# Strassen's scheme for the feed-forward down products: seven block products in place of eight

## The reference, cut to what matters

```python
def sq_relu_mlp(h, w_up, w_down):
    return jnp.square(jax.nn.relu(h @ w_up)) @ w_down
...
D_FF_2 = -(-8 * D_MODEL // (3 * 256)) * 256
```

## Time and profile before

| | |
|---|---|
| timed runs | 2347.6, 2345.95, 2345.96 us; median 2345.96 us |
| span of the profiled execution | 2345.8 us |
| TensorE busy | 2331.8 us (99%), 11493 matmuls |
| VectorE, ScalarE, GpSimd busy | 705.7, 935.1, 1079.8 us (30%, 40%, 46%) |
| chain that ended last | TensorE 96% |
| mean granted TensorE clock | 0.998 of 2.4 GHz |

### The profile page before, as it was taken

One profiled execution on the slowest core, in us unless ns is written; L12 is line 12 of the kernel. 1 busy time (PEld: TensorE's weight loads), 2 busy tenths in 40 slices (PEclk: granted clock), 3 DMA queues, 4 the chain that ended last, 5 costly groups with the idle time before them and its releaser, 6 DMA issues.

```text
span 2345.8 us, 29181 instructions
## 1 busy us (share of the span) xinstructions
PE 2331.8 (99%) x11493; PEld 1932.6 (82%) x11493; DVE 705.7 (30%) x1174; ACT 935.1 (40%) x1867; POOL 1079.8 (46%) x888
## 2 busy tenths in 40 slices
PE   9999999999999999999999999999999999999998
PEld 8888888888878888888887888888898778888887
DVE  3424320223474310323446321001242564100113
ACT  5525432333674432433446233223233662332331
POOL 5533644443535444544454354444454504544443
PEclk9999999999999999999999999999999999999999
DMA  6321333332303333323320243333333203433332
GB/s 189 86 63 54 117 99 95 99 96 72 99 30 108 102 99 95 99 92 92 93 89 32 91 132 94 101 97 98 91 104 77 75 1 91 129 101 95 99 96 75
DMA packets 156943, 213.73 MB, mean 91 GB/s; under 512 B 33615, under 2 KB 81479, under 8 KB 156807
## 3 DMA queue, kind: packets, MB, share of 16 engines
q1 hardware_dynamic: 153424, 203.24, 28.8%
q10 hardware_dynamic: 3383, 8.62, 1.2%
HBM read 209.18 MB, written 2.10 MB: 90 GB/s over the span
## 4 chain that ended last, share of the span: by engine, by line
PE 96%; DVE 1%; ACT 1%; issue 1%; POOL 0%; DMA 0%; SPq 0%; DVEq 0%; ACTq 0%; POOLq 0%
PE PS L343 45%; PE PS L345 40%; PE PS L1622 1%; PE PS L1600 1%; PE PS L463 1%; PE PS L2527 1%; PE PS L2514 0%; PE PS L1585 0%; PE PS L2119 0%; DVE X L594 0%; PE PS L1750 0%; PE PS L1150 0%; PE PS L444 0%; PE PS L1749 0%; PE PS L2518 0%
## 5 line engine op out<-in xcount | busy, mean ns | idle before, releaser
L318 POOL TENSOR_TENSOR WL<-WS,WH 128x512 fp32r<-128x512 f32 (+2 forms) x764 | 978.1, 1290 | 1063.5 <-ACT WH L307 1040.1
L307 ACT ACTIVATE WH<-WS 128x512 fp32r<-128x512 f32 (+2 forms) x766 | 473.2, 625 | 1167.4 <-PE PS L343 586.3
L343 PE MATMUL PS<-AH,WH 128*128 128x512 f32 (+1 forms) x1776 | 597.7, 369 | 1.3 <-ACT AH L480 1.3
L343 PE MATMUL PS<-AL,WH 128*128 128x512 f32 (+1 forms) x1776 | 593.5, 366 | 0.5 <-DVE AL L498 0.3
L343 PE MATMUL PS<-AH,WL 128*128 128x512 f32 x1584 | 586.8, 389 | 0.0
L343 PEld LDWEIGHTS PS<-AH,WH 128*128 128x128 f32 x1776 | 309.6, 188 | 57.4 <-issue 2.9
L343 PEld LDWEIGHTS PS<-AL,WH 128*128 128x128 f32 x1776 | 309.8, 189 | 55.7 <-DVE AL L498 0.8
L343 PEld LDWEIGHTS PS<-AH,WL 128*128 128x128 f32 x1584 | 296.9, 188 | 61.6
L345 PE MATMUL PS<-WH,h_HL 128*128 128x512 f32 x864 | 336.1, 389 | 0.0
L345 PE MATMUL PS<-WH,h_HH 128*128 128x512 f32 x864 | 336.1, 389 | 0.0
L345 PE MATMUL PS<-WL,h_HH 128*128 128x512 f32 x864 | 336.1, 389 | 0.0
(11 more groups left out here) (366 smaller groups left out, 1895.5 us busy)
## 6 DMA issues: line engine op xcount, KB each, us to landing
WS<-in_mlp_w_up_dram SPq DMA_DIRECT2D x128, 256.0 KB, 2.8
WS<-in_mlp_w_down_dram SPq DMA_DIRECT2D x128, 256.0 KB, 2.8
WS<-in_ffn_w_gate_dram SPq DMA_DIRECT2D x176, 128.0 KB, 2.1
WS<-in_ffn_w_up_dram SPq DMA_DIRECT2D x176, 128.0 KB, 2.2
WS<-in_ffn_w_down_dram SPq DMA_DIRECT2D x88, 256.0 KB, 2.6
WS<-in_gla_w_in_dram SPq DMA_DIRECT2D x48, 256.0 KB, 2.7
WS<-in_even_w_in_dram SPq DMA_DIRECT2D x48, 256.0 KB, 2.6
WS<-in_odd_w_in_dram SPq DMA_DIRECT2D x32, 256.0 KB, 2.6
```

The lines of the kernel that those rows point to most:

```text
L307: e.activation(WH[:, s, 0:n], WS[:, s, 0:n], ACT.Copy).then_inc(hi.sem, hi.tick(i))
L318: e.tensor_tensor(WL[:, s, 0:n], WS[:, s, 0:n], WH[:, s, 0:n].bitcast(F32), ALU.subtract).then_inc(lo.sem, lo.tick(i))
L343: return e.matmul(PS[b][0:mw, cs], weight[:, s, m * mw:(m + 1) * mw], x[:, cs], start=start, stop=stop, skip_group_check=head is not None)
```

## The change

The down products of the first 3072 hidden features of an MLP and of the first 2048 of an FFN are taken in chunks of 1024 features: 3 and 2 chunks. In a chunk the hidden features (a; 4 quarters of 256 tokens x 512 features) and the weights (b; 4 quarters of 512 rows x 512 columns) form a product of 2x2 blocks, and Strassen's scheme in Winograd's form takes seven products p1 to p7 of sums of them in place of eight. One product is 4 weight blocks x 2 token tiles x 3 matmuls. Some results are left in PSUM and the next product is added to them.

- The weights of a chunk are loaded as they are into a new area `hR` (16 blocks, semaphores `raw`), each as soon as the former chunk has freed its place. The stream has entries without a load (`mixed`) for the 28 blocks of a chunk; ScalarE and GpSimd take their source from `hR`, or from `WS` for p7. VectorE forms the weight differences (`dve_weight_sums`).
- The hidden features of a chunk stay in full precision. VectorE sums quarters (`dve_operand_sums`), ScalarE rounds an operand of 128 x 1024 (`act_op`), VectorE takes its rest (`dve_op`), into two buffers used in turn. Each is listed so that it follows the product two before.
- After each product VectorE adds its two banks to `Y` or `X` (`dve_summed`). In the MLP this was a copy by ScalarE, per column group and token tile.
- The seven products stand in one piece between up groups. MLP: groups 0, 1, 2, chunk 0, 3, 4, chunk 1, 5, two blocks of 6, chunk 2, the rest of 6, 7. FFN: groups 0 to 5, chunk 0, 6, 7, 8, chunk 1, 9, 10. The groups of one period use the same four banks, its products the other four. So in the FFN groups 4 and 5, and 6 and 7, follow each other in the same banks.
- The last 1024 features of an MLP and the last 768 of an FFN go through the same close as before, with 8 and 6 blocks for a column group in place of 16 and 10.

The core of the diff (left out: the buffers' places, the loads of a first chunk, GpSimd's lists, the parts of the MLP that answer to those shown of the FFN, the changed calls):

```diff
-        HH = take("HH", [P, 16, T], F32R)
-        HL = take("HL", [P, 16, T], F32R)
-        HT = take("HT", [P, 2, T])
+        hR = take("R", [P, 4, 4, RW])
...
+            for D, c, b, k in raw_at.get(i, ()):
+                raw_in(e, w, D, c, b, k)
+            if i in mixed:
+                return
...
                 w.wait_ge(mm, "used", i - NS)
+            if i in mixed:
+                source, *at = mixed[i]
+                w.wait_ge(*at)
+                e.activation(WH[:, s, 0:n], source, ACT.Copy).then_inc(hi.sem, hi.tick(i))
+                return
+            w.wait_ge(landed[s], i)
             e.activation(WH[:, s, 0:n], WS[:, s, 0:n], ACT.Copy).then_inc(hi.sem, hi.tick(i))
...
+            source = mixed[i][0] if i in mixed else WS[:, s, 0:n]
+            e.tensor_tensor(WL[:, s, 0:n], source, WH[:, s, 0:n].bitcast(F32), ALU.subtract).then_inc(lo.sem, lo.tick(i))
...
+        PRODUCTS = ("p1", "p7", "p6", "p4", "p5", "p2", "p3")
+        PLACE = {"p1": (0, 0), "p7": (2, 1), "p6": (2, 0), "p4": (2, 0), "p5": (2, 1), "p2": (0, 0), "p3": (0, 1)}
+        OPENS = ("p1", "p7", "p6", "p3")
+        FREED = {"p4": 0, "p5": 1, "p3": 3, "p2": 2}
...
+            def operand(self, q):
+                c, p = q // 7, PRODUCTS[q % 7]
+                if p in ("p6", "p5", "p3"):
+                    p6 = 7 * c + 2
+                    at = {"p6": (ve, "asum", self.name, p6), "p5": (ve, "asum", self.name, p6),
+                          "p3": (ve, "asum", self.name, 7 * c + 6)}[p]
+                    return self.quarter(c, 0, 1 if p == "p5" else 0), at
+                if p == "p7":
+                    return hZ, (ve, "asum", self.name, q)
+                if p == "p1":
+                    return self.quarter(c, 0, 0), self.made(c, 0)
+                return self.quarter(c, 1, 1 if p == "p4" else 0), self.made(c, 1)
...
+        WIDE = {8: (0, 1, 2, 3, 4, 5, 6)}
+        NARROW = {2: (0, 1, 2, 3, 4, 5, 6)}
+        LONG = {16: (0, 1, 2, 3, 4, 5, 6)}
...
+        def weight_source(D, c, p, k, i):
+            if p == "p7":
+                return WS[:, i % NS, :], ve, "wsum", D.name, c, p, k
+            if p in ("p6", "p4", "p5"):
+                return raw_tile(1 if p == "p5" else 0, k), ve, "wsum", D.name, c, p, k
...
+            i0, pair = first[D.name, c, p], banks[2:4] if p in ("p7", "p4", "p2") else banks[0:2]
+            w.wait_ge(ve, "op", D.name, q)
+            for k in range(4):
+                s = (i0 + k) % NS
+                w.wait_ge(lo, i0 + k)
+                for z in range(2):
+                    if k == 0 and held.get(pair[z]):
+                        w.wait_ge(*held[pair[z]])
+                    o, x = PS[pair[z]][:, :], slice(z * P, (z + 1) * P)
+                    xh, xl = D.oh[:, q % 2, k, x], D.ol[:, q % 2, k, x]
+                    e.matmul(o, xh, WH[:, s, :], start=k == 0 and p in ("p1", "p7", "p2"), stop=False, skip_group_check=True)
+                    e.matmul(o, xh, WL[:, s, :], start=False, stop=False, skip_group_check=True)
+                    m = e.matmul(o, xl, WH[:, s, :], start=False, stop=k == 3, skip_group_check=True)
+                    if k == 3:
+                        m.then_inc(mm.sem, mm.tick("product", D.name, q, z))
+                if k < 3:
+                    m.then_inc(mm.sem, mm.tick("used", i0 + k))
+                else:
+                    mm.name("used", i0 + k)
+            for z in range(2):
+                held[pair[z]] = (ve, "summed", D.name, q, z)
...
+        def act_op(e, w, D, q):
+            if q >= 7 * D.n:
+                return
+            source, at = D.operand(q)
+            w.wait_ge(*at)
+            if q >= 2:
+                w.wait_ge(mm, "product", D.name, q - 2, 1)
...
+        def dve_op(e, w, D, q):
+            if q >= 7 * D.n:
+                return
+            w.wait_ge(sc, "op", D.name, q)
+            e.tensor_tensor(D.ol[:, q % 2, :, :], D.operand(q)[0], D.oh[:, q % 2, :, :].bitcast(F32),
+                            ALU.subtract).then_inc(ve.sem, ve.tick("op", D.name, q))
...
+            a11, a21, a12, a22 = D.quarter(c, 0, 0), D.quarter(c, 0, 1), D.quarter(c, 1, 0), D.quarter(c, 1, 1)
+            if p == "p7":
+                w.wait_ge(*D.made(c, 0))
+                e.tensor_tensor(hZ, a11, a21, ALU.subtract).then_inc(ve.sem, ve.tick("asum", D.name, q))
+            elif p == "p6":
+                w.wait_ge(*D.made(c, 1))
+                e.tensor_tensor(a21, a21, a22, ALU.add).then_inc(ve.sem, ve.tick("s1", D.name, c))
+                w.wait_ge(ve, "s1", D.name, c)
+                w.wait_ge(ve, "op", D.name, 7 * c)
+                e.tensor_tensor(a11, a21, a11, ALU.subtract).then_inc(ve.sem, ve.tick("asum", D.name, q))
+            elif p == "p3":
+                w.wait_ge(ve, "op", D.name, 7 * c + 2)
+                e.tensor_tensor(a11, a12, a11, ALU.subtract).then_inc(ve.sem, ve.tick("asum", D.name, q))
...
+                for k in range(4):
+                    i = first.get((D.name, c, p), 0) + k
+                    w.wait_ge(raw[3][k], D.name, c)
+                    w.wait_ge(raw[1][k], D.name, c)
+                    w.wait_ge(lo, i - NS)
+                    e.tensor_tensor(WS[:, i % NS, :], raw_tile(3, k), raw_tile(1, k), ALU.subtract).then_inc(
+                        ve.sem, ve.tick("wsum", D.name, c, p, k))
+            elif p == "p6":
+                for k0 in (0, 2):
+                    b11, b12, b22 = (hR[:, b, k0:k0 + 2, :] for b in (0, 1, 3))
+                    for k in (k0, k0 + 1):
+                        w.wait_ge(raw[0][k], D.name, c)
+                        w.wait_ge(ve, "wsum", D.name, c, "p7", k)
+                    e.tensor_tensor(b12, b12, b11, ALU.subtract).then_inc(ve.sem, ve.tick())
+                    for k in (k0, k0 + 1):
+                        ve.name("wsum", D.name, c, "p5", k)
+                        w.wait_ge(lo, first.get((D.name, c, "p1"), 0) + k)
+                    w.wait_ge(ve, "wsum", D.name, c, "p5", k0)
+                    e.tensor_tensor(b11, b22, b12, ALU.subtract).then_inc(ve.sem, ve.tick())
+                    for k in (k0, k0 + 1):
+                        ve.name("wsum", D.name, c, p, k)
+            elif p == "p4":
+                for k0 in (0, 2):
+                    b11, b21 = hR[:, 0, k0:k0 + 2, :], hR[:, 2, k0:k0 + 2, :]
+                    for k in (k0, k0 + 1):
+                        w.wait_ge(raw[2][k], D.name, c)
+                        w.wait_ge(lo, first.get((D.name, c, "p6"), 0) + k)
+                    e.tensor_tensor(b11, b21, b11, ALU.subtract).then_inc(ve.sem, ve.tick())
+                    for k in (k0, k0 + 1):
+                        ve.name("wsum", D.name, c, p, k)
+        def dve_summed(e, w, D, q, banks):
+            p = PRODUCTS[q % 7]
+            pair, (t0, cg) = banks[2:4] if p in ("p7", "p4", "p2") else banks[0:2], PLACE[p]
+            for z in range(2):
+                t, b = t0 + z, PS[pair[z]]
...
+        def act_period(e, w, D, c, groups, order, closed):
+            for kind, k in walk(8 * len(groups), order):
+                if kind == "product":
+                    for j in range(4):
+                        weight_hi(e, w, first[D.name, c, PRODUCTS[k]] + j + NS)
+                    act_op(e, w, D, 7 * c + k + 2)
+                else:
+                    weight_hi(e, w, first[f"{D.name}.up{groups[k // 8]}", k % 8] + NS)
+                    if k % 8 == 7:
+                        closed(groups[k // 8])
...
+        def dve_period(e, w, D, c, groups, order, closed, banks):
+            late = None
+            for kind, k in walk(8 * len(groups), order):
+                if late is not None:
+                    dve_summed(e, w, D, late, banks)
+                    dve_op(e, w, D, late + 2)
+                    late = None
+                if kind == "product":
+                    late = 7 * c + k
+                    if k < 5:
+                        dve_weight_sums(e, w, D, late + 2)
+                    dve_operand_sums(e, w, D, late + 2)
+                else:
+                    if k == max(0, min(order) - 7):
+                        dve_weight_sums(e, w, D, 7 * c + 1)
+                    if k % 8 == 7:
+                        closed(groups[k // 8])
...
+        MLP_PERIODS = (((2, 3), WIDE), ((4, 5), WIDE), ((6,), NARROW))
+        def period_banks(c, o=0):
+            return ((BB, BA), (BA, BB))[(c + o) % 2]
...
+        FFN_PERIODS = (((4, 5, 6, 7), LONG), ((8, 9), WIDE))
...
+            for c, (groups, order) in enumerate(FFN_PERIODS):
+                b, banks = period_banks(c, layer)
+                for kind, k in walk(8 * len(groups), order):
+                    if kind == "product":
+                        pe_down(e, w, D, held, c, k, banks)
+                        continue
+                    g = groups[k // 8]
+                    pe_up(e, w, f"{name}.up{g}", src(g), k % 8, b, ready, held)
+                    if k % 8 == 7:
```

(25 more changed lines are left out.)

479 lines of the change are left out of this document (294 added, 185 removed).

## The result

The changed kernel takes 2410.14 us in the median of four runs (2408.97 to 2411.75), the kernel before 2345.95 us. The ratio is 1.0272, with an interval of 1.0258 to 1.0287: 64 us slower, where 2427 was predicted. The profiled execution has a span of 2410.0 us.

What follows compares the result with a forecast made beforehand. The kernel was taken as bound by its count of matmuls, as long as weight blocks are ready in time. Matmuls saved, chunk stalls and FFN bank waits summed as -54.4 + 129.0 + 6.8 = +81.4, giving 2427 us, range 2375 to 2465.

Steps and rivals of the forecast that it cites:

- 240 matmuls, 54.4 us: TensorE, ten chunks: each takes 168 matmuls instead of 192, 5.44 us less, 54.4 us in all.
- (a): Product weight blocks: each keeps TensorE 1.36 us, GpSimd needs 1.25 us, leaving it 8% slack instead of half.
- (b): VectorE per chunk: added sums, differences and operand rests from SBUF, taken as 1.22 us each at 1024 columns.
- (c): VectorE's two-SBUF-input instructions take turns with GpSimd's rests: 1.08 us behind a rest, 0.98 more for the next rest.
- Stall A: TensorE waits before p6 for VectorE's operand chain: 8.0 us in MLP chunks 0 and 1, 6.1 to 9.2 elsewhere.
- Stall B: TensorE waits before p4 for its operand rest: 3.9 us in MLP chunks 0 and 1.
- Stall C: Later waits before p3, in it and before the next up block: 2.1 us, 0.5 in a last chunk.
- (d): FFN groups following each other on the same banks wait for silu: 1.7 us, 4 times, 6.8 us.
- (e): Weight loads in the MLP's second group: cost 0; upper end 3 x 0.87 us once per MLP.
- 1 (no blocking): VectorE and GpSimd don't block each other, leaving the dependent chain before p6 and FFN bank waits: 2328 us, chance 0.09.
- 3 (the count alone): All operands are ready in time and only the FFN's same-bank waits remain: 2298 us, chance 0.02.
- 2 (the clock): TensorE's clock falls after each stall, costing 2 to 4 us a chunk: 2447 to 2467 us, chance 0.17.

Runs made afterwards that it cites:

- Kernel 9: Changed kernel with products spread singly between up blocks, later in the MLP, and MLP squares read from PSUM bank and ReLU: 2308.26 us, ratio 0.9834.
- kernel 2: Changed kernel with one SBUF input of VectorE's sums, differences and rests in the stretch read from idle PSUM, except MLP chunk 2: 2367.11 us, ratio 1.0085.
- kernel 4: Changed kernel with 28 extra matmuls (20 in the FFN's first chunk) between p7 and p6, except MLP chunk 2: 2424.15 us, ratio 1.0328.
- 1: Changed kernel with VectorE's six sums and differences for p6 listed in the up group ahead, behind p7's differences: 2365.88 us, ratio 1.0075.
- Kernel 3: Changed kernel with ScalarE's silus listed ahead of the rounding where an FFN group follows on the same banks: 2405.54 us, ratio 1.0248.
- 5: Changed kernel with the seven products put one by one between up blocks (closer in MLP chunk 2) instead of in one piece: 2321.64 us, ratio 0.9891.
- kernel 8: Changed kernel with p6's sums earlier, silu before rounding, MLP chunk 2 behind six up blocks, MLP squares from PSUM bank and ReLU: 2335.97 us, ratio 0.9954.
- kernel 6: As kernel 2, with 17 extra matmuls (4 in the FFN's first chunk) in front of p6, except MLP chunk 2: 2354.92 us, ratio 1.0034.

## Why the prediction was right, and where its sizes were off

The forecast of 2427 us was on the right side by the mechanism it named, and 17 us too high. Some of that nearness is luck: 8.1 us of slower pace, which it did not have, stand against terms that came out 25 us smaller in sum. Of its two signs, 8 and 4 us of waiting at the third and the fourth product, only the first was seen. Step by step:

- **240 matmuls, 54.4 us.** Right: the count of operand loads is 11,253. Kernel 9 shows that this gain can be had almost whole.
- **(a), (b), the pace of preparation.** Right. The length I had to bracket, VectorE on 1024 columns from SBUF, is 1.22 to 1.23 us; I took 1.22.
- **(c), the turns.** Right, as the earlier trace rows had shown it, and kernel 2 settles it. I had VectorE end 1.08 us behind the rest that it waits for: its instruction of 303.82 ends 1.07 us behind GpSimd's of 301.63, that of 310.68 1.09 behind GpSimd's of 308.20. By the Trainium skill, page "SBUF — State Buffer", section "SBUF: two separate sides", whichever of the two engines starts first keeps the shared pair for its whole instruction; kernels 2 and 4 agree, with VectorE's 1.22 against 2.24 us and with the near tie, in which one of the two engines keeps its own length (1.21 or 1.27 us) and the other is held up.
- **Stall A.** Forecast 8.0 us in MLP chunks 0 and 1, 6.4 in MLP chunk 2, 6.1 and 9.2 in the FFN's; measured 7.29, 6.36, 5.09 and 7.92. In sum 67.9 for 75.4. Kernels 1 and 2 show its two causes, each alone: with the sums in another place it is 17.7 us in all, without the turns 39.6. The whole time falls by 46 and by 44 us, other waits included; the two overlap and don't add up.
- **Stall B.** The step that failed: 39.0 us forecast, 3.2 measured, with 27.2 of low clock where I had said it costs nothing. The prediction did say that a fall of the clock behind A lies in front of stall B and is hidden by it, and kernel 4 bears that out: take the low clock away and B is back, 3.5 us for a forecast of 3.9. The changed kernel's own chunks show it too: in the six in which 8 to 11 matmuls of p6 are slow, p4 starts 8.0 us behind p6 every time. Where 13 or 14 are, it starts 8.25 to 8.5 us behind it in three, so there the low clock just outlasts B; and 9.2 us in the fourth, where VectorE lost its turn. But the sum of both was to be 39.0 and is 30.4. The operand of p4 was forecast for 28.2 us behind p1 and is there at 26.3 in the first chunk. Half a microsecond of this comes from A; for the rest, I had VectorE wait a turn of GpSimd's for the rest of p4's operand, and in this kernel it won that tie (1.21 us, where kernel 4 shows 2.32).
- **Stall C.** 14.6 forecast, 6.6 measured, and at another place: 0.3 and 0.6 us before the second and the fourth weight block of p2, for GpSimd's rest. There is no wait over 0.3 us before p3, in it or before the next up block. So the kind of wait was right, and its place and size were not.
- **(d).** 1.46 us each instead of 1.7: the three durations of the forecast, 0.26 + 0.63 + 0.58, without the 0.1 for each signal, which no run shows. Kernel 3 removes these waits.
- **(e), the loads.** Right at 0: the first matmuls of up blocks wait for the silus of (d) and for nothing else.
- **Not foreseen.** Product matmuls start every 0.2310 and 0.2335 us instead of every 0.2267: 8.1 us here, and 8 to 9 us in each kernel for which I added it up (2, 5 and 9).

The rivals: 1 (no blocking) is refuted; kernel 2 had to take the turns away to come to its wait of 3.4 us before p6 (4.2). 3 (the count alone) gave 2298; kernel 9 shows what it takes to get within some 10 us of it. 2 (the clock) needs the most care. The clock fell each time, as it said and as the Trainium skill's page "TensorE: Matmul & The Clock Gate", section "Why this matters for your kernels", warns. Yet it didn't add 20 to 40 us to the forecast, because slow matmuls cost time only if their successor could have started: in the changed kernel p4's operand was late anyway.

## What to carry over

When a scheme saves matmuls by adding sums, compare the pace, not the shares: how long each weight block keeps TensorE busy (here 1.36 us, 2.72 before) against what the other engines need for it, in the densest stretch and not over the kernel. The same seven products cost 64 us in one piece and gained 26 us when they were only spread among blocks that leave the helpers half idle, 39 with the squares moved off the shared path as well. The piece need not be a loss either: kernel 8 keeps it together and gains 11 us, by the order of the helpers' lists, a later place for MLP chunk 2 and the squares from PSUM. An operand that comes from PSUM instead of SBUF keeps a two-input VectorE instruction out of GpSimd's way.

## What the runs showed of the hardware

- A filled stall is not a gain by itself: the dummy matmuls of kernel 4, where the operand behind them was late anyway, came with 13 us more (about 9 of them from that operand's later coming), and a like filling saved 12 us in kernel 6, where it was not late.
- The cost of the low clock behind a wait varies where the wait does not: in the changed kernel, behind waits of 7.3 us before p6, it held for 3.5 to 5.7 us, with matmuls 0.43 us apart (8 to 13 of them), and behind the 5.1 us in the FFN for 5.7 and 6.1.
- A VectorE instruction on 128x1024 takes the same 1.22 us with both inputs from SBUF as with one from PSUM, as long as GpSimd is idle.
- The product matmuls' slower pace follows the stage: in the MLPs most of it is at the change from one group of three to the next (0.2356 us there, 0.2283 to 0.2289 within), in the FFNs it is even (0.2333 to 0.2337). It is there in kernels 2, 5 and 9 alike, in which the other engines do quite different things beside it, and not in the down products left as they were, which start every 0.2268 us in the same kernel. What causes it was not tried and stays open.
